# Filler products on TensorE ahead of two waits of the attention loop

## The reference

```
s = einsum("bqhcd,bkhcd->bhcqk", q_blk, k) * scale + bias      # c = 0, 1: two score maps a head, 64 deep
s = where(rel >= 0, s, -inf)                                   # causal
p = softmax(s, axis=-1)
a = p[:, :, 0] - lam * p[:, :, 1]
o = einsum("bhqk,bkhe->bqhe", a, v)                            # 128 wide
o = rms_norm(o, subln_g) * (1 - lambda_init);  y = o @ w_o
```

## Time and profile before

| | us |
|---|---|
| time, median of 3 runs | 1715.71 (1714.29 to 1717.42) |
| time of the profiled execution | 1716.73 |
| span of the profiled execution | 1714.9 |
| mean granted clock of TensorE | 0.973 of full |
| PE busy | 1617.2 (94%) |
| DVE busy | 1157.3 (67%) |
| ACT busy | 785.2 (46%) |

### The profile page before, as it was taken

One profiled execution on the slowest core, in us unless ns is written; L12 is line 12 of the kernel. 1 busy time (PEld: TensorE's weight loads), 2 busy tenths in 40 slices (PEclk: granted clock), 3 DMA queues, 4 the chain that ended last, 5 costly groups with the idle time before them and its releaser, 6 DMA issues.

```text
span 1714.9 us, 33143 instructions
## 1 busy us (share of the span) xinstructions
PE 1617.2 (94%) x12174; PEld 1515.5 (88%) x12174; DVE 1157.3 (67%) x1795; ACT 785.2 (46%) x1377; POOL 389.6 (23%) x398
## 2 busy tenths in 40 slices
PE   3999899999988999999998999999999999999997
PEld 2998799998975899998787989977999989889997
DVE  6897889999966688746656442236777465587754
ACT  3555465644456555643682222225444445544342
POOL 0000234412000233303024553202433020143311
PEclk8999999999986999999998999998999999999998
DMA  8442557797740365653241000003466534335661
GB/s 330 176 173 97 209 186 241 240 388 316 246 148 2 98 187 183 215 175 135 86 147 51 2 1 1 1 1 98 152 191 195 197 123 135 122 120 187 190 214 62
DMA packets 68142, 258.14 MB, mean 151 GB/s; under 512 B 7512, under 2 KB 9696, under 8 KB 67552
## 3 DMA queue, kind: packets, MB, share of 16 engines
q1 hardware_dynamic: 68064, 257.10, 44.7%
HBM read 256.01 MB, written 1.06 MB: 150 GB/s over the span
## 4 chain that ended last, share of the span: by engine, by line
PE 69%; DVE 17%; issue 6%; DMA 4%; ACT 3%; POOL 1%; DVEq 0%; SPq 0%; ACTq 0%; POOLq 0%
PE ps L534 17%; PE ps L535 16%; PE ps L536 16%; DMA modraw<-in_wmod 4%; PE ps L503 3%; PE ps L786 3%; PE ps L803 2%; DVE lo L1352 2%; PE ps L801 2%; DVE modraw L1358 2%; DVE inv L1383 2%; DVE Y L1389 1%; PE ps L495 1%; DVE tmp L1554 1%; PE ps L826 1%
## 5 line engine op out<-in xcount | busy, mean ns | idle before, releaser
L534 PE MATMUL ps<-OH,lo 128*128 128x256 f32 x2176 | 625.8, 288 | 25.1 <-DVE OL L1405 11.0
L1352 DVE TENSOR_TENSOR lo<-raw,hi 128x1024 fp32r<-128x1024 f32 (+1 forms) x350 | 480.0, 1388 | 207.6 <-ACT hi L952 206.1
L535 PE MATMUL ps<-OL,hi 128*128 128x256 f32 x2176 | 616.2, 283 | 0.0
L536 PE MATMUL ps<-OH,hi 128*128 128x256 f32 x2176 | 611.2, 281 | 0.0
L534 PEld LDWEIGHTS ps<-OH,lo 128*128 128x128 f32 x2176 | 413.1, 190 | 47.8 <-issue 19.0
L536 PEld LDWEIGHTS ps<-OH,hi 128*128 128x128 f32 x2176 | 414.0, 190 | 0.0
L535 PEld LDWEIGHTS ps<-OL,hi 128*128 128x128 f32 x2176 | 413.0, 190 | 0.6
L952 ACT ACTIVATE hi<-raw 128x1024 fp32r<-128x1024 f32 (+1 forms) x350 | 380.6, 1110 | 46.5 <-DMA raw<-in_w 43.6
L534 PE MATMUL ps<-GH,lo 128*128 128x256 f32 x704 | 198.8, 282 | 2.6 <-DVE lo L1352 2.5
L535 PE MATMUL ps<-GL,hi 128*128 128x256 f32 x704 | 198.1, 281 | 0.0
L536 PE MATMUL ps<-GH,hi 128*128 128x256 f32 x704 | 198.1, 281 | 0.0
(11 more groups left out here) (306 smaller groups left out, 2259.8 us busy)
## 6 DMA issues: line engine op xcount, KB each, us to landing
raw<-in_w SPq DMA_DIRECT2D x288, 512.0 KB, 3.9
modraw<-in_wmod SPq DMA_DIRECT2D x96, 512.0 KB, 5.4
raw<-in_w SPq DMA_DIRECT2D x64, 704.0 KB, 5.3
l<-in_lora_in SPq DMA_DIRECT2D x1, 1536.0 KB, 6.4
l<-in_lora_out SPq DMA_DIRECT2D x1, 1536.0 KB, 9.7
con_sb<-in_con SPq DMA_DIRECT2D x1, 1046.5 KB, 7.2
X<-in_xin SPq DMA_DIRECT2D x1, 1024.0 KB, 6.6
biasrev<-rel_bias_rows SPq DMA_DIRECT2D x1, 1024.0 KB, 5.9
```

Source lines behind the costliest of these rows:

```text
L534: pe.matmul(bank[:, 0:T], lo[:, r, w], oh[:, k0 + k], start=first, stop=False)
L535: pe.matmul(bank[:, 0:T], hi[:, r, w], ol[:, k0 + k], start=False, stop=False)
L536: ins = pe.matmul(bank[:, 0:T], hi[:, r, w], oh[:, k0 + k], start=False, stop=final)
L1352: dve.tensor_tensor(lo[:, s, 0:kt * P], raw[:, s, 0:kt * P], hi[:, s, 0:kt * P].bitcast(F32), ALU.subtract).then_inc(lo_made, 1)
```

## The change

In each iteration two calls of `keep_busy` are put into PE's queue: one ahead of the wait for the probabilities (9 products at the first step, 3 at each of the 15 others, into the bank that the transposes write next), one ahead of the wait for the transposed copies (1 product at each of the 16 steps, into the bank that the values products write next). For that the wait that the bank is free moves ahead of the filler. Nothing else changes.

```
                 if 1 <= n <= NA:
                     m = n - 1
+                    wait(pe, S("aT_copied"), m - 1)
+                    keep_busy(3 if m else 9, 4 + m % 2)
                     pe.wait_ge(S("att_probs"), m + 1)
                     if m == 1:
                         pe.wait_ge(S("lam_ready"), 1)
-                    wait(pe, S("aT_copied"), m - 1)
                     for kb in range(m % 2 + 1):
...
                 if n >= 2:
                     m = n - 2
+                    wait(pe, S("o_copied"), m - 1)
+                    keep_busy(1, 6 + m % 2)
                     pe.wait_ge(S("aT_copied"), m + 1)
-                    wait(pe, S("o_copied"), m - 1)
                     for kb in range(m % 2 + 1):
```

## The result

The changed kernel is slower: 1725.57 us median (1722.55 to 1728.78) beside 1715.0 us (1712.37 to 1717.73) for the kernel before on the same chip, a ratio of 1.0061 with a 95% interval of 1.0045 to 1.0077. The forecast was 1728.4 us, in a range of 1721.7 to 1733.7.

A forecast was written before the change was run, and what follows sets the result against it. PE, at full clock, was to become the bound through 70 added products; opening +3.3, loop +10.4, end of loop +0.9 and square sums -1.95 gave +12.7 us on the median 1715.7, so 1728.4 us, range 1721.7 to 1733.7.

The forecast's parts named there:

- Rival A: Attention: filler fills only idle time, the clock stays full and DVE sets the pace; -6.5 us, 1709.2 us; chance 3%.
- Rival B: Attention: added products overlap with their neighbours, 4.8 us a pair; -0.2 us, no change; chance 5%, including other ways there.
- Rival C: Whole kernel: slower by less than the forecast range, +3.4 to +6 us, loop at 5.4 us a pair; chance 5%.
- D: Attention: the clock stays at half although PE is full, pair near 12 us, +50 us; chance 2%.
- The opening: From scores(2) to the first transpose: nine products delay it, +3.3 us if the clock falls, +1.8 if it holds.
- The loop: First to fifteenth transpose, seven pairs of steps: each pair 6.1 us instead of 4.61, +10.4 us.
- The 5.87 us that the rows summed to: One pair of steps in the loop: PE's groups with filler, back to back at full clock, priced from the trace.
- four further changes between groups: One pair of steps: about 0.06 us at each change between groups not within the priced figures, making 6.1 us.
- The end of the loop: From the fifteenth transpose to the square sums: 4.7 us instead of 3.77, +0.9 us.
- The square sums: After the attention loop: 16 records at full clock instead of partly half, 5.52 us before, -1.95 us.
- the second dip: Clock fall after the square sums, 549.2 to 556.0 us: expected again at another place, 0, bounds -2.1 and +2.1 us.
- lower bound for a pair: One pair of steps in the loop: 5.05 us with all PE records without any gap.

The follow-up runs named there:

- Experiment 7: Changed kernel with 4 filler products instead of 3 ahead of each of 15 steps; 1733.65 us in one profiled execution.
- Experiment 2: Changed kernel with all 70 filler products 128 columns wide instead of 256; ratio 0.9967 to the kernel before.
- Experiment 1: Changed kernel with both `keep_busy` lines left out, so only the waits moved; ratio 1.0002 to the kernel before.
- Experiment 9: Changed kernel with 2 products between scores(1) and scores(2), 4 ahead of the first probabilities, 1 at later steps, none ahead of values products; ratio 0.9972 to the kernel before.
- experiments 4: Changed kernel with only the single product ahead of the values products, none ahead of the probabilities; ratio 0.9985 to the kernel before.
- experiment 5: Changed kernel with filler only ahead of the probabilities, 5 products at the first step and 1 at each other; ratio 0.9978 to the kernel before.
- experiment 3: Changed kernel without the single product ahead of the values products, keeping 9, then 3 ahead of the probabilities; ratio 1.0005 to the kernel before.
- second set: The changed kernel timed once more, instruction for instruction; ratio 1.0039 to the kernel before.
- experiment 6: As experiment 5, plus one 128-column filler product in each of the five spread products that wait for DVE; ratio 1.0007 to the kernel before.
- experiment 8: Changed kernel with 5 filler products at the first step instead of 9; 1720.21 us in one profiled execution.

## Why the prediction was right, and where it was off

**The mechanism held.** PE became the bound (48.38 of 48.40 us busy), the waits for the probabilities are gone, DVE waits for scores instead, the clock is full, the filler has 140 records more at 0.216 us (the prediction's (2.75 - 0.38) / 11 is 0.2155 and not 0.2157, which changes no later figure). Experiment 7 adds two products a pair, and the pair grows by 0.86 us, the price of two. Experiment 2 halves the columns of 16 records, and the pair shrinks by 1.67 us, 0.104 a record where half the price is 0.108. Price times count accounts for the loss to within 0.06 us a pair. Experiment 1 excludes the moved waits. Rival A, the filler that is free, is not this kernel. Its condition was a product under 0.245 us. Experiment 2 meets it, with about 0.21 us for a product of 128 columns: -0.33%, about -4.4 us at the medians, against the -6.5 it was given. Experiment 9 comes to the same, -0.28% and -4.5 us, with products of 0.43 us but two a pair in place of eight. What a product costs is thus not all that decides; so do how many there are and where they stand (experiments 4 and 5, 4.39 and 4.12 us a pair).

Rival B (overlap with neighbours) fell by the 0.216 us of a record. Rival C (+3.4 to +6 us, 5.4 us a pair) fell less clearly: the profiles and both sets of timings have +6.8 us or more, but the mean pair, 39.80 / 7 = 5.69 us, lies halfway between it and the forecast. D did not occur: wherever PE was full in the loop the clock stayed up, and where experiment 3 had the clock fall in the opening with PE full it was back after 3.4 us.

**The size was too high by 5 us, in three terms, all the same way.** The opening: +3.3 taken, +1.75 measured. The other end of that term's range, +1.8, was the right one for both profiles of this program. Experiments 3 and 7, with the same nine products, had the clock fall, for +3.38 and +3.36, so both prices were fair, and which of them an execution pays was not to be known: that part of the miss is chance. The loop: +10.4 taken, +7.56 measured. The 5.87 us that the rows summed to was near (5.90 measured), in part by luck: the two bursts were priced 0.06 us too high each (1.46, measured 1.40) and the two groups of scores 0.09 too low each (0.33 and 0.54, measured 0.42 and 0.63). The 0.06 us at each of four further changes between groups, added by judgement, did not exist, 7 x 0.2 = 1.4 us. The rest, 1.5 us, is a slip of counting: the first pair lacks the values stage and its filler (5.02 us), the last the scores (5.28), and only five pairs of seven are full. The end of the loop: +0.9 taken, +0.36 measured, because its bursts, with no scores ahead of them, took 1.30 us and not 1.46, and for the same surcharge. The square sums came as forecast, and the second dip moved without changing its length (6.8 us both times).

The median of the first set, +10.6 us over before, lies nearer to the forecast than the profiled attention does, but that agreement is not worth much: the second set has +6.8, and executions differ by where the clock falls in and before the attention, which one profile doesn't tell.

## What to carry to other kernels

Filler that keeps an engine's clock up is work, and on an in-order queue whatever stands behind it pays for it, save where the engine would have waited anyhow. So sum it for one period of the loop with the engine's own work at the full clock, and compare that with the pace of the engine that sets the period, not with the idle time at the low clock. Put it directly ahead of a wait for that engine, behind the products that this engine itself waits for; the same two products a pair cost 0.27 us in one place and none in the other. Here two products a pair, a quarter of what was put in, held the clock, and nine products in an opening with 2.18 us of idle time put off the loop by 1.75 us, or by 3.4 where the clock fell.

## What was not expected of the hardware

- Filler, transposes and values products, all of 128 rows, followed each other in the kernel after at the price of their records (0.11 us of 128 columns, 0.216 of 256). Around the scores, of 64 rows, that is not so. In the rows of the kernel after, the values products ahead of scores take 514.54 - 514.22 = 0.32 us and the burst behind them 1.40; at the end of the loop, where no scores stand between the two, they take 0.22 and 1.30. With every record back to back, and the scores two by two, the prediction's lower bound for a pair was 5.05 us; 5.90 were measured, and the 0.85 us between them lie at and in the two groups of scores. In the spread of experiment 6, with records of 8 and of 128 rows in turn at half clock, a step took 1.87 us for 1.28 us of records.
- In the spread of the kernel after PE was busy without a gap from 555.4 to 557.6 us, behind a wait of 0.47 us; then the clock fell, and stayed at 0.50 for 6.80 us in which PE was busy throughout. In experiment 9 it stayed full through 35 us of the loop, where PE was busy for 84% of the time with 0.86 us of filler in a pair of 4.12.
- Two executions of nearly the same opening, with the same first products, had the clock fall in one (experiment 5) and not in the other (experiment 8). With nine products it fell in experiments 3 and 7 and in neither profile of the changed kernel.
